# Conditioning pieces moved between places of the program, and 16 of them multiplied by GpSimd instead of TensorE

## What is computed

```
mod_x = (jax.nn.silu(c) @ w_ada + b_ada)[:, None, :]
mod_c = jax.nn.silu(c_ctx) @ w_ada + b_ada
sh1x, sc1x, g1x, sh2x, sc2x, g2x = jnp.split(mod_x, 6, axis=-1)
hx = modulate(rmsnorm(x, norm1_g), sh1x, sc1x)
```

## Time and profile before

| | |
|---|---|
| time, median of 3 runs | 2678.23 us |
| profiled execution | 2673.65 us |
| its span, first to last instruction | 2671.8 us |
| TensorE busy | 2407.6 us (90%) |
| VectorE, ScalarE busy | 1244.9 (47%), 968.5 (36%) |
| GpSimd busy | 279.7 (10%), nearly all indirect loads |
| read from HBM | 881 MB, mean 330 GB/s |
| mean granted TensorE clock | 0.983 of full speed |

### The profile page before, as it was taken

One profiled execution on the slowest core, in us unless ns is written; L12 is line 12 of the kernel. 1 busy time (PEld: TensorE's weight loads), 2 busy tenths in 40 slices (PEclk: granted clock), 3 DMA queues, 4 the chain that ended last, 5 costly groups with the idle time before them and its releaser, 6 DMA issues.

```text
span 2671.8 us, 43703 instructions
## 1 busy us (share of the span) xinstructions
PE 2407.6 (90%) x16386; PEld 1583.0 (59%) x16386; DVE 1244.9 (47%) x3088; ACT 968.5 (36%) x2098; POOL 279.7 (10%) x273
## 2 busy tenths in 40 slices
PE   7989989999999999999898998987877877789997
PEld 5769965555544555555487897442222322488997
DVE  2544542222222222222234666766666665556783
ACT  3444331122211111221223445444344344545762
POOL 0000000000000000000000001444444444100000
PEclk9999999999999999999999999999999999999999
DMA  6766599999999998999937556999999999533552
GB/s 262 271 261 236 219 379 422 422 422 422 422 422 422 422 422 328 422 422 422 409 133 303 217 193 238 421 421 421 421 421 421 421 421 421 204 140 111 190 179 106
DMA packets 121587, 884.03 MB, mean 331 GB/s; under 512 B 13552, under 2 KB 13552, under 8 KB 14192
## 3 DMA queue, kind: packets, MB, share of 16 engines
q1 hardware_dynamic: 83232, 606.11, 56.6%
q0 software_dynamic: 38224, 276.13, 24.9%
HBM read 881.14 MB, written 1.05 MB: 330 GB/s over the span
## 4 chain that ended last, share of the span: by engine, by line
PE 53%; DMA 21%; ACT 5%; DVE 3%; issue 2%; SPq 2%; POOL 0%; ACTq 0%; DVEq 0%; POOLq 0%
PE psum L1080 13%; DMA work<-in_uv,work 12%; PE psum L804 10%; PE psum L1446 8%; PE psum L1112 6%; DMA work<-in_stream 6%; DMA weight_ring<-in_stream 3%; PE psum L1525 2%; PE psum L1047 2%; PE psum L1026 2%; SPq L1580 2%; ACT work L3004 1%; ACT work L2606 1%; PE psum L823 1%; PE psum L791 1%
## 5 line engine op out<-in xcount | busy, mean ns | idle before, releaser
L1446 PE MATMUL psum<-work 128*128 128x512 f32 x1024 | 505.7, 626 | 120.7 <-ACT work L3004 119.8
L1446 PEld LDWEIGHTS psum<-work 128*128 128x128 f32 x1024 | 181.8, 193 | 437.5 <-ACT work L3004 279.4
L2373 DVE CUSTOM_DVE_ANT_0 work<-work 128x1024 f32<-128x1024 f32 x256 | 313.7, 1225 | 220.8 <-DMA work<-in_uv,work 220.3
L1080 PE MATMUL psum<-work 128*64 128x256 f32 x3168 | 366.2, 382 | 15.3 <-DMA work<-in_stream 15.0
L2017 DVE TENSOR_TENSOR work<-psum,work 128x256 f32<-128x256 f32 x132 | 56.1, 425 | 690.1 <-PE psum L1058 690.1
L1656 DVE TENSOR_TENSOR ring_parts<-weight_ring,peer_parts 128x1024 fp32r<-128x1024 f32 x218 | 262.6, 1222 | 235.2 <-ACT peer_parts L2662 191.2
L2662 ACT ACTIVATE peer_parts<-weight_ring 128x1024 fp32r<-128x1024 f32 x218 | 224.9, 1053 | 245.2 <-PE psum L804 99.7
L3169 POOL DMA_INDIRECT work<-in_uv,work x256 | 272.3, 1064 | 394.1 <-PE psum L1446 351.5
L1080 PEld LDWEIGHTS psum<-work 128*64 128x64 f32 x3168 | 219.6, 137 | 153.0 <-DMA work<-in_stream 31.8
L1112 PE MATMUL psum<-weight_ring,work 128*64 128x512 f32 x1056 | 244.6, 599 | 29.1 <-ACT work L2830 25.2
L2812 ACT ACTIVATE work<-psum 128x256 f32<-128x256 f32 x132 | 50.7, 384 | 366.2 <-PE psum L1080 366.2
(11 more groups left out here) (331 smaller groups left out, 3193.6 us busy)
## 6 DMA issues: line engine op xcount, KB each, us to landing
weight_ring<-in_stream SPq DMA_DIRECT2D x322, 1024.0 KB, 7.7
work<-in_stream SPq DMA_DIRECT2D x192, 1024.0 KB, 22.5
chunkbuf<-in_stream SPq DMA_DIRECT2D x64, 1024.0 KB, 22.4
work<-in_uv,work POOLq DMA_INDIRECT x256, 22.7
work<-in_rows POOLq DMA_DIRECT2D x1, 1312.0 KB, 14.4
xT<-in_x POOLq DMA_DIRECT2D x1, 1024.0 KB, 11.4
work<-in_ctx POOLq DMA_DIRECT2D x1, 1024.0 KB, 9.3
work<-in_keys POOLq DMA_DIRECT2D x1, 1024.0 KB, 6.2
```

The lines of the kernel that those rows point to most:

```text
L1080: mm = pe.matmul(psum[g * SEATS:(g + 1) * SEATS, 4 + i % 2, 0:256], m["xe"][:, 4 * h + c, odd * SEATS:(odd + 1) * SEATS], w[:, c, g, :], s ...
L1446: mm = pe.matmul(psum[:, 2 * t + h, :], m["diag"][:, g % DIAGS, :], m["rows_of_uv"][row_place[g]][:, D + h * 512:D + (h + 1) * 512], start ...
L2373: ve.tensor_tensor_reduce(row, row, m["h_nat"][:, t, :], 1.0, 0.0, ALU.mult, ALU.add, m["score"][:, g:g + 1]).then_inc(pick_s, 1)
```

## The change

Some pieces of the conditioning move to other places, and 16 are computed in another way.

- Attention 1 has one piece in each of its 16 steps (ada1:8 to 23); ada2:0 and 1 go into drain step 17, ada2:2 into 18, ada2:3 behind the last values. `u1` and `out1` have none.
- ada3:0 to 3 lie behind `q2` instead of `hq`; ada3:14 and 15 in the drain steps 9 and 10 of attention 2 instead of steps 6 and 7.
- ada2:4 to 19 (`ASIDE`) leave the ring. GpSimd brings each in two halves of 512 KB through its own queue, multiplies a half by silu(c) as a column repeated 256 times, adds the chunks up in pairs, and adds the halves. What is left of a piece is 512 columns in one of three buffers. TensorE adds them over the partitions by two matmuls of 256 columns with a column of ones (`lanes`), at the places that `LANES` lists.
- SyncE starts loads of expert slots 1, 4 and 5 only when ada2:19 is done (their memory is used by the new buffers), and slot 1 no longer ahead of `out1`.
- ScalarE's copy of the row `mod1b` waits for ada2:3 instead of ada2:7.

```diff
-BESIDE = {("attn1", p): [] for p in range(16)}
-for k in range(24):
-    BESIDE["attn1", 2 * (k // 3) + k % 3 // 2].append((1, 8 + k, 9 + k) if k < 16 else (2, k - 16, k - 15))
-for i in range(4):
-    BESIDE["u1", i] = [(2, 8 + 2 * i, 10 + 2 * i)]
-for i in range(4):
-    BESIDE["out1", i] = [(2, 16 + i, 17 + i)]
+BESIDE = {("attn1", p): [(1, 8 + p, 9 + p)] for p in range(16)}
+BESIDE["attn1", 17] = [(2, 0, 2)]
+BESIDE["attn1", 18] = [(2, 2, 3)]
+BESIDE["attn1", 19] = [(2, 3, 4)]
...
-    BESIDE["hq", i] = [(3, 2 * i, 2 * i + 2)]
+    BESIDE["q2", i] = [(3, 2 * i, 2 * i + 2)]
...
-    BESIDE["attn2", p] = [(3, 8 + p, 9 + p)]
+    BESIDE["attn2", p + 3 * (p > 5)] = [(3, 8 + p, 9 + p)]
+
+ASIDE = [(2, j) for j in range(4, 20)]
+LANES = {("q1", 0): 1, ("q1", 1): 1, ("q1", 3): 1, ("attn1", 0): 1, ("attn1", 2): 1, ("attn1", 5): 1, ("attn1", 7): 1,
+         ("attn1", 10): 1, ("attn1", 12): 1, ("attn1", 15): 1, ("u1", 0): 1, ("u1", 1): 1, ("u1", 3): 1,
+         ("pooled", 3): 1, ("ga", 0): 1, ("ga", 2): 1}
...
+            def lanes(E, *key):
+                for _ in range(LANES.get(key, 0)):
+                    g = len(given)
+                    s, j = ASIDE[g]
+                    given.append(g)
+                    if key == ("u1", 0):
+                        pe.wait_ge(*at("row:mod1b"))
+                    pe.wait_ge(*at(f"aside:{g}"))
+                    for k in range(2):
+                        q = STRIP * (2 * (g % 2) + k)
+                        mm = pe.matmul(psum[q:q + STRIP, 7, 256 * (s == 2):256 * (s == 2) + 256],
+                                       lane[:, STRIP - 1 - j:WINDOW - j], aside_sum[g % SUMS][:, k, :],
+                                       start=(g < 2), stop=True, skip_group_check=True)
+                    mm.then_inc(*E.up(f"ada{s}:{j}"))
...
-                row("mod1b", 0, "ada2:7", 0, A_)
+                row("mod1b", 0, "ada2:3", 0, A_)
...
+                for s in (1, 2):
+                    gp.wait_ge(*at(f"csil{s}:{int(s == 1)}"))
+                gp.wait_ge(*at("ada1:7"))
+                load(0, 0)
+                load(0, 1)
+                for g, (s, j) in enumerate(ASIDE):
+                    sums = aside_sum[g % SUMS]
+                    if g >= SUMS:
+                        gp.wait_ge(*at("ada{}:{}".format(*ASIDE[g - SUMS])))
+                    for e in range(2):
+                        gp.wait_ge(aside_in[e], 16 * (g + 1))
+                        silu = strips[s][:, 4 * e:4 * e + 4, STRIP - 1:STRIP].to_broadcast([P, 4, 256])
+                        gp.tensor_tensor(aside_half[e], aside_half[e], silu, ALU.mult).then_inc(*G.up())
+                        gp.wait_ge(*G.now())
+                        gp.tensor_tensor(aside_half[e][:, 0:2, :] if e else sums, aside_half[e][:, 0:2, :],
+                                         aside_half[e][:, 2:4, :], ALU.add).then_inc(*G.up())
+                        gp.wait_ge(*G.now())
+                        if e:
+                            gp.tensor_tensor(sums, sums, aside_half[e][:, 0:2, :], ALU.add).then_inc(*G.up(f"aside:{g}"))
+                        if g + 1 < len(ASIDE):
+                            if e:
+                                gp.wait_ge(*G.now())
+                            load(g + 1, e)
```

More of the change, by code:

```diff
@@ L122, in order @@
             if name == "u1":
-                for p in range(16):
+                for p in range(20):
                     beside("attn1", p)
@@ L130, in order @@
                     if part == "attn2":
-                        for p in range(8):
+                        for p in range(12):
                             beside("attn2", p)
@@ L140, in order @@
                 beside(name, i)
-    assert len(set(got)) == len(got) == sum(k for _, k in PIECES)
+    assert len(set(got + ASIDE)) == len(got) + len(ASIDE) == sum(k for _, k in PIECES)
     return got
@@ L322, in build @@
         moe_in = sem("moe_tables_in")
+        aside_in = [sem(f"aside_half_in_{e}") for e in range(2)]
+        aside_half = [work[:, ASIDE_AT + e * D:ASIDE_AT + e * D + D].rearrange("p (c o) -> p c o", o=256) for e in range(2)]
+        aside_sum = [(work[:, SUMS_AT + k * 512:SUMS_AT + k * 512 + 512] if k < 2 else chunkbuf[:, 8, :])
+                     .rearrange("p (k o) -> p k o", k=2) for k in range(SUMS)]
+        lane = work[:, LANE_AT:LANE_AT + WINDOW]
         x_in = sem("x_in")
@@ L941, in attention @@
                         scores(s, i, E, m)
-                        beside(f"attn{s}", i)
+                    beside(f"attn{s}", i)
+                    lanes(E, f"attn{s}", i)
                     if s == 3:
@@ L948, in attention @@
                         turn(s, i - 2, E, m)
+                beside(f"attn{s}", pairs + 3)
             def drain():
@@ L1587, in _ @@
                 begin(0)
-                begin(1)
                 sent(out_at, moe_at, 0)
                 sp.wait_ge(used.sem, out_at + 1)
-                begin(4)
-                begin(5)
+                sp.wait_ge(*at("ada2:19"))
+                for j in (1, 4, 5):
+                    begin(j)
                 sp.wait_ge(*at("out1:3"))
@@ L3186, in shapes @@
     n -= 12
-    got = {"stream": (n, P, SLOT), "x": (P, DC, T), "vec": (P, sum(V_LEN[s] for s in stages)), "ident": (P, P)}
+    got = {"aside": (len(ASIDE), P, SLOT)} if 1 in stages else {}
+    got.update({"stream": (n, P, SLOT), "x": (P, DC, T), "vec": (P, sum(V_LEN[s] for s in stages)), "ident": (P, P)})
     if 1 in stages:
@@ L3378, in in_order @@
         n += 12 * E_N if name == "moe" else k
[L3379 removed]
+    return whole[[at[f"ada{s}"] + j for s, j in ASIDE]], whole[[at[name] + i for name, i in order() if name != "moe" or i < 12 * E_N]]
 def arrays(a, stages):
     W = {s: {1: layout1, 2: layout2, 3: layout3}[s](a) for s in stages}
[L3384 removed]
+    aside, stream = in_order([p for s in stages for p in W[s]["stream"]])
+    got = {"in_stream": stream, "in_aside": aside,
            "in_x": turned(a["x"][0]), "in_vec": np.concatenate([v for s in stages for v in W[s]["vec"]], 1),
```

30 lines of the change are left out of this document (23 added, 7 removed).

## The result

The changed kernel takes 2690.09 us (median of 6 runs, 2687.2 to 2695.7) against 2677.4 us of the kernel before beside it (6 runs). The ratio is 1.0048, 95% interval 1.0034 to 1.0063: **slower by some 13 us**, where 2672.8 was forecast. The profiled execution took 2695.7 us, 5.6 above the median, so the two traces are 22 us apart where the medians are 13.

A forecast was written before the change was run, and what follows sets the result against it. TensorE was taken to bound both mixers and transfers the stretch from 350 us. First mixer -12.1, second +0.6 and GpSimd's cost to others +6.1 gave -5.4: 2672.8 us on the median, 8-in-10 range 2664 to 2690.

The forecast's parts named there:

- What bounds the kernel, and that the first mixer's time passes on one for one: TensorE binds the first mixer, transfers from 350 us; time saved up to out1's last piece shifts everything behind equally.
- The first mixer without contention, -12.1: Start through out1: fewer pieces and waits, minus added lanes, save 12.1 us if GpSimd delays nobody.
- -6.9: Attention 1: its 16 pairs take 16 single pieces instead of 24 pieces, 16.0 us instead of 22.9.
- +0.75: End of attention 1: ada2:0 and 1 cost 0.75 us net of a wait; ada2:2 and 3 hide in waits.
- Lanes at 0.45: Two TensorE matmuls of 256 columns per GpSimd piece, 0.45 us each time, 16 times: +7.2 us (4.0 to 8.0).
- GpSimd's piece at 9.7 us: One conditioning piece on GpSimd: arithmetic at twice VectorE's time, 8.6 us, plus 1.1 for issues.
- rival 3: First mixer: GpSimd too slow, TensorE waits at lanes; decides from 12.7 us a piece; 2688 us, chance 0.14.
- What GpSimd's work costs the others, +6.1: Attention 1 and its two ends: GpSimd delays VectorE's chain, forecast at 6.1 us.
- half of 9.6 and 1.3 for both ends: Half of attention 1's full-exclusion cost of 9.6 us, plus 1.3 for ropes ahead and VectorE's small steps behind.
- rival 2: Attention 1: VectorE becomes the bound as its small steps wait for GpSimd instructions; pairs 5.5 us, 2685.7 us, chance 0.24.
- ck and cv, -4.3: Second mixer: moving ada3:0 to 3 behind q2 removes weight waits of 3.47 and 2.41 us; net 4.3 saved.
- End of attention 2, +4.9: TensorE resumes 4.9 us later, since ScalarE makes the late hg:1's high halves before copying the last turned probabilities.

The follow-up runs named there:

- Experiment 1: Changed kernel with GpSimd's five operations per piece cut to 4 columns of each chunk instead of 256; 2669.0 us, 0.998 of the kernel before.
- experiments 4: Changed kernel with each GpSimd operation cut into instructions of 256 columns, same elements; 2689.64 us, 1.0067 of the kernel before.
- 6: Changed kernel with GpSimd starting only at the end of attention 1, taking twelve pieces, ada2:8 to 19; 2676.59 us, 1.0003 of the kernel before.
- experiment 10: Changed kernel with GpSimd's five operations per piece replaced by one-input multiplications by 0.5, same element count; 2679.24 us, 1.0014 of the kernel before.
- experiment 5: Changed kernel run again, unedited, against the kernel before; 2692.62 us, 1.0068.
- the first trace: Profiled execution of the unedited changed kernel in its first comparison with the kernel before; 2695.7 us.
- experiment 8: Changed kernel with ScalarE copying attention 2's last turned probabilities before making hg's high halves; 2682.5 us, 1.0029 of the kernel before.
- experiment 3: Changed kernel with both second-mixer moves undone (ada3:0 to 3 and ada3:14 and 15); 2686.33 us, 1.0048 of the kernel before.

## Why the prediction was wrong, step by step

- **What bounds the kernel, and that the first mixer's time passes on one for one: right.** 985 us from `out1` to the second mixer in both traces, whatever came ahead.
- **The first mixer without contention, -12.1: nearly right, some 3 us too much.** Experiment 1 is that case. Attention 1 took 81.4 us instead of 83.4 (-2.0; the terms -6.9, +0.75 and seven lanes give -3.0), u1 to `out1` 159.2 instead of 170.3 (-11.1; the terms give -10.5), u1's waits vanished as said. All together -9.3: the front was 3.8 later, of which its three lanes are 1.4 to 1.7 and the rest is within the 2 us to which one trace tells it.
- **Lanes at 0.45: a little low.** Start to start, a lane takes 0.56:

```profile
83.92 0.62 PE L699 MATMUL psum<-work 128*32 128x256 f32 x4
84.48 1.12 PE L889 MATMUL psum<-work 128*128 128x512 f32 x2
```

- **GpSimd's piece at 9.7 us: right, by luck.** Its rows in the changed kernel sum to 136.2 us of arithmetic for 16 pieces, 8.5 each, and two issues of 0.59 make 9.7. But by its undisturbed rows (1.92 and 1.27) a piece would be 7.6 and 1.2, so 8.8, 1.6 to 1.8 times VectorE's time per element, not twice; the rest is time that VectorE kept it waiting. TensorE never waited for GpSimd at a lane there, so rival 3 was wrong for this kernel; experiments 4, 6 and 10 show it becoming true when a piece passes the spacing of the lanes. They also show that its threshold of 12.7 us was drawn with all three buffers and all the slack counted in.
- **What GpSimd's work costs the others, +6.1: wrong, and this is the step that failed.** The text took "half of 9.6 and 1.3 for both ends". The runs show 18 to 24 us, the price of **rival 2** (16 and 3). Its mechanism is what the rows show, though not for each step: a two-input step or a scaling that meets a running GpSimd instruction waits to its end, and the next one slips in between. A step of attention 1 costs 5.6 to 5.9 us, predicted there as 5.5: (98.35 - 81.39)/16 = 1.06 more than in experiment 1 by experiment 5, 1.4 by the first trace, on 4.5. The text's own sign for rival 2, pairs above 5.2, came true. The halving had no row behind it. It averaged two outcomes, when the arithmetic of the text already said that with exclusion 3.8 us had to fit beside 2.9 in 4.5. And the ends were not 0 to 2 each. The front lost 3 to 7 us, because the low halves of q1 and the whole rope arithmetic, not the last rope alone, run beside GpSimd; the text named only the ropes ahead of the first pair. The clock came on top of both: each of the waits of 2.75 to 5.29 us shown above for attention 1 was followed by matmuls at half speed.

The Trainium skill (*SBUF — State Buffer*, Who interferes with whom) had stated this lock, and the trace of the changed kernel agrees: steps with two SBUF inputs grew from 1226 to 2380 ns, the same operation with one input in PSUM stayed at 0.68 us, the maximum from PSUM at 1.22, and two scalings in SBUF grew from 0.88 to 4.14. Its rule is an exclusion for whole instructions; the prediction put half its price into the forecast and gave rival 2, the full one, a chance of 0.24. For GpSimd instructions with one input the rule does not hold as stated: in experiment 10 two-input steps ran at 0.15 us inside an instruction of 2.78 us, and the measurement decides.

- **ck and cv, -4.3: too much.** The mechanism holds (ck no longer waits), the sum does not. From the opening of the second mixer to attention 2 the changed kernel gained 1.4 us. ck's own row was 3.57 us because it ran at half clock behind its wait (granted clock 0.51 from 1408.5 to 1411.9); without the wait it runs at 1.00 and takes 2.03. So it hides 1.5 us less of the landing of cv:1 than the text let it ("ck hides 3.5 of it"), and hf, kept late by the same ring, gave back 1.2.
- **End of attention 2, +4.9: right in place, mechanism and size of the wait** (5.10, with ScalarE 5.34 for the ring before it; the last values come 4.89 later behind the first scores), and experiment 8 shows the cause by removing it. Left out was the clock behind such a wait: the stretch grew by 7.0 us in the first trace, and its removal gave 8.7 in experiment 8, by chance somewhat more than the wait had cost, and 3 to 5 in experiment 3, where the clock fell elsewhere.
- **The sum by what was measured**: -9 to -11 for the first mixer, -1.4 and +7 in the second, +18 to +24 for the lock, so +13 to +21; measured +13 and +18. The range's upper end, 2690, was called rival 3's, whose sum does not come out evenly: 2678.2 + 12 is 2690, the text has 2688. It had no term for the clock in it, and the measured 2690.09 lies just above it.

## What to carry to other kernels

Arithmetic on two SBUF tensors that is moved to GpSimd was not moved to an idle engine here: price it as a VectorE task that can't be interrupted, and look at whether VectorE's chain is awaited by others, not at VectorE's busy share. Where two outcomes of an unknown are far apart, forecast the one whose mechanism fits the rows, not their mean. A wait put in front of TensorE costs itself and, as with the waits of 3 to 5 us here, a stretch at half clock behind it; and a row read behind a wait may be such a stretch (ck: 3.57 us behind its wait, 2.03 without). And look for holes first: here the four pieces put where TensorE stood anyway, and those behind q2, gave 0.35% without any second engine (some of it unexplained), and one line of ScalarE's program moved behind another gave 0.4% of the changed kernel.
